# The gate's projection as seven half-size products over both halves of the tokens

## The chip, the cores and the metric

One core of a Trainium2 chip runs the whole kernel. The metric is the time of one execution in microseconds, median of several runs. Its engines are TensorE (PE), VectorE (DVE), ScalarE (ACT), GpSimd (POOL) and SyncE (SP), which here only issues transfers; each has its own instruction stream and they meet at semaphores.

## The reference

One layer of a decoder over 1024 tokens of 2048 features, in float32. Cut to what matters here:

```python
y = jnp.concatenate([y_h, y_g], axis=-1) @ w_out[i]
h = h + y.astype(dtype)

e = rms_norm(p[i] @ ple_proj[i], ple_norm_w[i])
gate = jax.nn.sigmoid(rms_norm(h, ple_gate_norm_w[i]) @ ple_gate_w[i] + ple_gate_b[i])
h = h + (gate * e).astype(dtype)
return rms_norm(h, final_norm_w)
```

Ahead of it stand an input projection and two groups of linear-attention heads. The change is in the last four lines: the projection with `ple_gate_w` (2048 x 2048), the gate, and the final norm.

## The kernel before

The tokens are worked on in two halves of 512; activations lie feature by feature, as tiles of 128 features x 512 tokens. `tile(h, c)` is tile c (of 16) of half h: in `feat` for half 0, in `work` for half 1. A product in float32 accuracy is made of three in a rounded format: both operands are split into a high part (by ScalarE: `split_weights`, `fill_high`) and a low part (by VectorE: `low_weights`, `fill_low`), and `passes` issues low x high, high x low, high x high. The operands stand in `act_hi`/`act_lo` and, twice, in `w_hi`/`w_lo`.

Weights come in slabs of 1 MB, in two transfers of 512 KB that SyncE issues (`load_slab`), each as soon as `low_weights` of the same half of the slab before has freed `w_raw[j]`. A slab is 16 x 3 = 48 products of 512 columns. The code of VectorE and ScalarE has in each iteration the splitting of the next slab first and then the work on the present one. The order on every engine is that of the code; SyncE's loads are in a written order too, so that a load which must wait holds up all behind it.

The output projection (`OUT_SLABS = 28`) is already made of seven half-size matrix products over both token halves (P1, P2, P5, P6, P7, P4, P3, four slabs each; a slab is two parts of 24 products, each into its own bank of four, `out_banks`). GpSimd makes the sums of weight blocks (`w_sums`) and of activations (`t_sums`) by transfers that add to their destination. `out_part` combines on VectorE; `x_part` brings in the residual from x tiles that SyncE loads (`load_x_tile`); `out_square` on ScalarE and `out_end` on VectorE add up the squares. `row_factors` makes a factor per token from these sums, at slabs 21, 25 and 27.

The gate's projection is 2 x 16 whole slabs, `g_pair` on TensorE: half 0, then half 1, one tile of logits per slab. For each tile VectorE runs `g_first` and `g_rest` (multiply by the row factor, add the bias, weights' low part, log-sigmoid with ScalarE's Abs, Exp, Ln and Exp, multiply by e, add to h, which stands in the tile, scale, add the square). SyncE loads e ahead (`load_e`), one slab early. The loops over half 1 scale half 0's tiles (`f_scale`) and store them (`store_out`). The last slab is made in two half-width parts; the tail (`z_...`) finishes it, makes the factors of half 1 and scales and stores that half, six tiles of it by token through TensorE's transposes.

## Time and profile before

| | us |
|---|---|
| median of 3 runs (2191.51 to 2192.65) | 2192.04 |
| span of the profiled execution, first to last instruction | 2189.4 |
| TensorE busy in it | 2175.6 |
| VectorE busy | 1520.5 |
| ScalarE busy | 1014.7 |

The profile's span leaves out what lies around the instructions; no time of its own is listed for the profiled execution, so its span is set against the median. A busy share is a mean over all stages. Start times count from the span's start; overlapping instructions of one kind in a row are merged, so that a price is best read as the distance between two starts.

### The profile page before, as it was taken

The numbers are of one execution on the slowest core, as the hardware profiler recorded it, in microseconds if no ns is written. First come the engines' busy times: TensorE is split into PE (matmuls) and PEld (weight loads), VectorE is DVE, ScalarE is ACT, GpSimd is POOL, SyncE is SP. The second block draws the span as 40 slices with busy tenths as digits, with TensorE's granted clock in tenths as the row PEclk, the third lists the DMA queues.
The fourth block names the chain that finished last, engine by engine and source line by source line (L and its number), as shares of the span: only waits on it lengthen the run. The fifth ranks groups of instructions, "written<-read, shape, count | busy, mean of one in ns | idle before, by whom it ended". The sixth has DMA issues, their size and how long they took to land.

```text
span 2189.4 us, 30587 instructions
## 1 busy us (share of the span) xinstructions
PE 2175.6 (99%) x10418; PEld 1821.7 (83%) x10418; DVE 1520.5 (69%) x3019; ACT 1014.7 (46%) x1759; POOL 96.8 (4%) x148
## 2 busy tenths in 40 slices
PE   9999999999999999999999999999999999999997
PEld 8888888888888888888888888888888888888886
DVE  7577777775666577766667565557667777768886
ACT  7454545444334354444445343335354445446554
POOL 1001011110000000000000000000110000000000
PEclk9999999999999999999999999999999999999998
DMA  9435665565432322232322545335576543332443
GB/s 338 170 102 163 171 178 168 165 177 145 125 99 86 97 69 87 85 126 81 115 99 93 173 152 141 98 108 145 187 250 235 173 163 115 121 123 98 159 161 127
DMA packets 100015, 310.27 MB, mean 142 GB/s; under 512 B 11360, under 2 KB 16736, under 8 KB 99168
## 3 DMA queue, kind: packets, MB, share of 16 engines
q1 hardware_dynamic: 88288, 248.42, 33.7%
q0 software_dynamic: 11648, 60.83, 10.9%
q8 instruction: 46, 0.75, 0.1%
q14 instruction: 33, 0.27, 0.0%
HBM read 284.04 MB, written 75.50 MB: 164 GB/s over the span
## 4 chain that ended last, share of the span: by engine, by line
PE 98%; DVE 1%; ACT 1%; issue 0%; DVEq 0%; ACTq 0%
PE acc L740 27%; PE acc L742 27%; PE acc L741 27%; PE lv L833 3%; PE so L842 1%; PE so L845 1%; PE so L822 1%; PE ms L742 1%; PE ms L741 1%; PE ms L740 1%; PE ms L811 1%; PE tr L741 1%; PE tr L742 1%; PE tr L740 1%; PE tr L857 0%; PE tr L807 0%
## 5 line engine op out<-in xcount | busy, mean ns | idle before, releaser
L740 PE MATMUL acc<-act_hi,w_lo 128*128 128x512 f32 (+1 forms) x2656 | 1063.0, 400 | 0.7 <-DVE work L2058 0.7
L742 PE MATMUL acc<-act_hi,w_hi 128*128 128x512 f32 (+1 forms) x2656 | 1033.9, 389 | 0.0
L741 PE MATMUL acc<-act_lo,w_hi 128*128 128x512 f32 (+1 forms) x2656 | 1033.4, 389 | 0.0
L742 PEld LDWEIGHTS acc<-act_hi,w_hi 128*128 128x128 f32 x2656 | 498.6, 188 | 104.9
L740 PEld LDWEIGHTS acc<-act_hi,w_lo 128*128 128x128 f32 x2656 | 499.7, 188 | 99.2 <-issue 3.9
L741 PEld LDWEIGHTS acc<-act_lo,w_hi 128*128 128x128 f32 x2656 | 500.0, 188 | 95.5 <-issue 1.7
L1049 ACT CAST w_hi<-w_raw 128x1024 fp32r<-128x1024 f32 x347 | 350.7, 1048 | 444.1 <-PE acc L742 357.5
L1537 DVE TENSOR_TENSOR w_lo<-w_raw,w_hi 128x1024 fp32r<-128x1024 f32 x347 | 410.7, 1220 | 104.4 <-ACT w_hi L1049 101.2
L1121 ACT ACTIVATE work<-work 128x512 f32<-128x512 f32 x120 | 75.7, 630 | 148.2 <-DVE work L1593 147.4
L1063 ACT ACTIVATE work<-work 128x512 f32<-128x512 f32 x95 | 60.1, 632 | 136.8 <-DVE work L1573 136.8
L1607 DVE COPY_PREDICATED work<-mask_sb,lv 128x256 f32<-128x256 uint8 x168 | 88.8, 529 | 7.3
L833 PEld LDWEIGHTS lv<-work 128*128 128x128 f32 x480 | 71.9, 190 | 9.4
L1599 DVE TENSOR_TENSOR work<-work 128x256 f32<-128x256 f32 x120 | 50.9, 424 | 39.4 <-ACT work L1121 39.3
L833 PE MATMUL lv<-work 128*128 128x128 f32 x480 | 72.6, 273 | 0.0
L1059 ACT ACTIVATE work<-work 128x512 f32<-128x512 f32 x103 | 65.2, 633 | 3.3
L1057 ACT ACTIVATE work<-work 128x512 f32<-128x512 f32 x103 | 65.2, 633 | 3.3
L1521 DVE MEMSET vec_dummy<- 128x1 f32 x230 | 13.6, 59 | 68.2 <-PE lv L833 63.5
L1578 DVE SCALAR_TENSOR_TENSOR work<-acc,work 128x512 f32<-128x512 f32 x48 | 33.2, 692 | 33.8 <-ACT work L1063 33.8
L1149 ACT ACTIVATE work<-work 128x128 f32<-128x128 f32 (+1 forms) x96 | 32.0, 334 | 41.5 <-DVE work L1642 41.5
L1593 DVE TENSOR_TENSOR work<-work 128x256 f32<-128x256 f32 x120 | 50.3, 419 | 0.0
L1592 DVE TENSOR_TENSOR work<-work 128x256 f32<-128x256 f32 x120 | 50.2, 419 | 0.0
L1600 DVE TENSOR_TENSOR work<-work 128x256 f32<-128x256 f32 x120 | 50.2, 418 | 0.0
(323 smaller groups left out, 2186.8 us busy)
## 6 DMA issues: line engine op xcount, KB each, us to landing
w_raw<-in_slabs SPq DMA_DIRECT2D x316, 512.0 KB, 4.5
w_sums<-in_slabs POOLq DMA_DIRECT2D x48, 512.0 KB, 6.3
w_raw<-w_sums SPq DMA_DIRECT2D x32, 512.0 KB, 4.2
work<-e_scratch SPq DMA_DIRECT2D x56, 256.0 KB, 2.8
t_sums<-y_scratch POOLq DMA_DIRECT2D x24, 512.0 KB, 6.8
feat<-in_x_feat SPq DMA_DIRECT2D x8, 1024.0 KB, 11.7
e_scratch<-work SPq DMA_DIRECT2D x32, 256.0 KB, 5.9
w_sums<-w_sums POOLq DMA_DIRECT2D x16, 512.0 KB, 3.9
```

The lines of the kernel that those rows point to most:

```text
L740: nc.tensor.matmul(ps, lhs_lo, rhs_hi, start=start, stop=False)
L741: nc.tensor.matmul(ps, lhs_hi, rhs_lo, start=False, stop=False)
L742: return nc.tensor.matmul(ps, lhs_hi, rhs_hi, start=False, stop=stop)
L833: last = nc.tensor.matmul(scores[:, :, c * half:(c + 1) * half], x_lv[l % 3][:, c * C:(c + 1) * C], queries[:, :, c * half:(c + 1) * half] ...
L1049: nc.scalar.copy(w_hi[par][:, j, :], w_raw[j][:, :]).then_inc(w_hi_ready, 1)
L1057: st.mark(A(t1, t1, ACT.Exp, scale=-1.0))
L1059: A(t1, t1, ACT.Ln, bias=1.0).then_inc(sp_ready, 1)
L1063: A(t2, t2, ACT.Exp).then_inc(sig_ready, 1)
L1121: A(x_lv[l % 3], x_lv[l % 3], ACT.Exp).then_inc(lv_exp, 1)
L1537: v.tensor_tensor(w_lo[par][:, j, :], w_raw[j][:, :], w_hi[par][:, j, :].bitcast(F32), ALU.subtract).then_inc(w_lo_ready, 1)
L1599: st.mark(v.tensor_tensor(keys, keys, lower_tokens(k_t, s), ALU.mult))
L1607: v.copy_predicated(upper_tokens(attn, s), mask_sb[:, l, :].rearrange("p (b n s) -> p b n s", b=2, s=s), lv_ps[l % 2][:, 0:TH // 2].rearra ...
```

## The change

The gate's projection becomes seven half-size products over both token halves as well: 28 slabs (`GATE_SLABS`) of two parts, in the order P1, P2, P1, P2 (two slabs each), then P6, P7, P5, P4, P3 (four each). A P2 slab finishes two tiles of half 0 (c below 8), P5 two of half 1 (c from 8), P4 two of half 0, P3 two of half 1; P1, P6 and P7 finish none. Weight sums for it (`weight_sums(1, c)`) are made by GpSimd during the input projection. The row factor is applied to the logits as before.

The tile of h is no longer kept in SBUF: as a tile of h is finished in the output projection, SyncE stores it (`keep_h`), ScalarE then multiplies it in place by the norm weight with a sign (`sign_tile`), and SyncE stores this too (`store_signed`); GpSimd makes four groups of sums of it (`G1` to `G4`). The gate loads these sums (`load_gate_t`, three buffers) and, for every tile, e and h (`load_tile`, two buffers). The gate's sigmoid is one Sigmoid with the bias in it, in place of four functions; ScalarE loads another function table for it and back for the row factors. The final scaling of half 0 and its sixteen stores stand behind the gate's loop; the final norm's weight is applied there instead of tile by tile.

```diff
+GATE_PARTS = ([(P1, 0), (P1, 1), (P2, 0), (P2, 1), (P1, 2), (P1, 3), (P2, 2), (P2, 3)]
+              + [(what, i) for what in (P6, P7, P5, P4, P3) for i in range(4)])
+def gate_tile(n, j):
+    what, i = GATE_PARTS[n]
+    c = 2 * i + j
+    return {P2: (0, c), P5: (1, HK + c), P4: (0, HK + c), P3: (1, c)}.get(what)
...
+            def keep_h(q):
+                h, c, n, j = OUT_TILES[q]
+                sp.wait_ge(out_free[out_place(n, j)], out_done(n))
+                if q >= 4:
+                    sp.wait_ge(*tile_stored(q - 4))
+                sp.dma_start(h_kept[h, c], (feat, work)[h][:, c, :]).then_inc(h_out[q % 4], 16)
+            def store_signed(q):
+                h, c = OUT_TILES[q][0:2]
+                sp.wait_ge(hs_ready, q + 1)
+                sp.dma_start(h_signed[h, c], (feat, work)[h][:, c, :]).then_inc(h_out[q % 4], 16)
+            def load_tile(q):
+                h, c = G_TILES[q][0:2]
                 if q >= 2:
-                    sp.wait_ge(e_used, q - 1)
-                sp.dma_start(e_in[c % 2], e_scratch[q]).then_inc(e_loaded[c % 2], 16)
+                    sp.wait_ge(g2_sum, q - 1)
+                sp.dma_start(e_in[q % 2], e_scratch[h * KT + c]).then_inc(e_loaded[q % 2], 16)
+                sp.dma_start(h_in[q % 2], h_kept[h, c]).then_inc(e_loaded[q % 2], 16)
+            def load_gate_t(a, k):
+                u = gate_use(a, k)
+                if k == 0 and a != 24:
+                    sp.wait_ge(gt_summed[a - 20], HK // 2 * 16)
+                if u >= 3:
+                    sp.wait_ge(act_lo_ready, FILL_NO[21] + u - 2)
+                src = h_signed[1, HK + k] if a == 24 else t_sums[a - 16, k]
+                sp.dma_start(gate_t[u % 3], src).then_inc(gt_loaded[u % 3], 16)
...
-                if n == 25:
-                    sp.wait_ge(act_lo_ready, fill_no(14, HK - 1))
-                    load_e(0, 0)
-                    load_e(0, 1)
+                for j in range(2):
+                    if (n - 1, j) in ENDS_AT:
+                        keep_h(ENDS_AT[n - 1, j])
+                for j in range(2):
+                    if (n - 2, j) in ENDS_AT:
+                        store_signed(ENDS_AT[n - 2, j])
                 load_slab(S_OUT + n + 3)
-            for h in range(HALVES):
-                for c in range(KT):
-                    if h * KT + c + 2 < 2 * KT:
-                        load_e(h + (c + 2) // KT, (c + 2) % KT)
-                    if s_gate(h) + c + 3 < SLABS:
-                        load_slab(s_gate(h) + c + 3)
-                    if h and 2 <= c < 10:
-                        store_out(0, 2 * c - 4)
-                        store_out(0, 2 * c - 3)
+            sp.wait_ge(logit_ready, HALVES * NG)
+            sp.wait_ge(glr_ready, HALVES)
+            sp.wait_ge(act_lo_ready, fill_no(14, HK - 1))
+            for n in range(GATE_SLABS):
+                if n == 0:
+                    for q in (30, 31):
+                        keep_h(q)
+                    for q in (28, 29, 30, 31):
+                        store_signed(q)
+                for j in range(2):
+                    if (n, j) in G_NO:
+                        load_tile(G_NO[n, j])
+                if n + 1 < GATE_SLABS:
+                    for a, k in GATE_FILLS_AT[n + 1]:
+                        load_gate_t(a, k)
+                if n == 4:
+                    sp.wait_ge(copied, 2 * HK * 64)
+                    sp.wait_ge(summed, 2 * HK * 64)
+                if n + 3 < GATE_SLABS:
+                    load_slab(S_GATE + n + 3)
+            for n in range(KT):
+                store_out(0, n)
+            T0, T1 = TOKEN_FIRST, TOKEN_FIRST + N_TOK
...
+            for c in range(HK // 2):
+                pool.wait_ge(y_stored, (HK + c) * 16 + 32)
+                weight_sums(1, c)
...
+            pairs = range(0, HK, 2)
+            for c in pairs:
+                hs_there(0, c)
+                g.dma_start(flat(G1, c, 2), flat(h_signed[0], c, 2)).then_inc(gt_copied, 16)
+            for c in pairs:
+                hs_there(1, c)
+                g.dma_start(flat(G3, c, 2), flat(h_signed[1], c, 2)).then_inc(gt_copied, 16)
+                pool.wait_ge(gt_copied, HK // 2 * 16 + c // 2 * 16 + 16)
+                add_to(flat(G1, c, 2), flat(h_signed[1], c, 2)).then_inc(added1, 16)
+            pool.wait_ge(added1, HK // 2 * 16)
+            for c in pairs:
+                g.dma_start(flat(G2, c, 2), flat(G1, c, 2)).then_inc(gt_copied, 16)
+            for c in pairs:
+                hs_there(1, HK + c)
+            pool.wait_ge(gt_copied, 3 * HK // 2 * 16)
+            for c in pairs:
+                add_to(flat(G2, c, 2), flat(h_signed[1], HK + c, 2)).then_inc(added2, 16)
+            for c in pairs:
+                add_to(flat(G3, c, 2), flat(h_signed[1], HK + c, 2)).then_inc(added3, 16)
+            pool.wait_ge(added2, HK // 2 * 16)
+            for c in pairs:
+                g.dma_start(flat(G4, c, 2), flat(G2, c, 2)).then_inc(gt_copied, 16)
+            for c in pairs:
+                hs_there(0, HK + c)
+            pool.wait_ge(gt_copied, 4 * HK // 2 * 16)
+            for c in pairs:
+                add_to(flat(G4, c, 2), flat(h_signed[0], HK + c, 2)).then_inc(added4, 16)
...
+            def sign_tile(n, j):
+                q = ENDS_AT[n, j]
+                h, c = OUT_TILES[q][0:2]
+                act.wait_ge(*tile_kept(q))
+                scale = (pgn if (h == 0) == (c < HK) else pgn_neg)[:, c:c + 1]
...
                 if (n - 1, 1) in ENDS_AT:
                     out_square(n - 1, 1)
+                    sign_tile(n - 1, 0)
                 if (n, 0) in ENDS_AT:
                     out_square(n, 0)
                 if out_slab(n)[0] in (P1, P5):
                     for j in range(2):
                         out_copy(n, j)
+                if (n - 1, 1) in ENDS_AT:
+                    sign_tile(n - 1, 1)
...
+            def g_sigmoid(q):
+                h, c = G_TILES[q][0:2]
+                act.wait_ge(logit_at, q + 1)
+                A(sig[q % 2], tile(h, c), ACT.Sigmoid, bias=g_vec[:, 3 * c:3 * c + 1]).then_inc(sig_ready, 1)
+            def g_square(q):
+                h, c = G_TILES[q][0:2]
+                act.wait_ge(g2_sum, q + 1)
+                A(sq[q % 2], tile(h, c), ACT.Square).then_inc(g2_sq, 1)
+                if h == 1 and TOKEN_FIRST <= c < TOKEN_FIRST + N_TOK:
+                    A(tile(h, c), tile(h, c), ACT.Copy, scale=g_vec[:, 3 * c + 2:3 * c + 3]).then_inc(fw_ready, 1)
+            for n in range(GATE_SLABS):
+                after = G_NO.get((n - 1, 1))
+                if n + 1 < GATE_SLABS and n:
+                    split_weights(S_GATE + n + 1, (n + 1) % 2, (0,))
+                if after is not None:
+                    g_sigmoid(after)
+                if n + 1 < GATE_SLABS and n:
+                    split_weights(S_GATE + n + 1, (n + 1) % 2, (1,))
+                if after is not None:
+                    g_square(after)
+                if n in (2, 27):
+                    act.preload_act_table_set("natural_log_exp_and_others")
+                    if n == 2:
+                        row_rsqrt(ROWS_H[1], r_h[1], h_sum[1])
+                    else:
+                        row_rsqrt(ROWS_F[0], f_r[0], g_sum[0])
+                    act.preload_act_table_set("sigmoid_and_others")
+                for a, k in GATE_FILLS_AT[n]:
+                    fill_high(a, k)
+                if GATE_PARTS[n][0] == P1:
+                    for j in range(2):
+                        p1_copy(n, j)
+                if (n, 0) in G_NO:
+                    g_sigmoid(G_NO[n, 0])
+                    g_square(G_NO[n, 0])
                 st.fresh()
...
+            def g_logits(n, j):
+                q = G_NO[n, j]
+                h, c = G_TILES[q][0:2]
+                vec_e.wait_ge(out_free[gate_place(n, j)], gate_freed(n))
+                st.wait()
+                v.tensor_tensor(tile(h, c), tile(h, c), r_h[h], ALU.mult).then_inc(logit_at, 1)
+            def g_embed(q):
+                h, c = G_TILES[q][0:2]
+                vec_e.wait_ge(e_loaded[q % 2], q // 2 * 32 + 32)
+                st.mark(v.scalar_tensor_tensor(out=e_in[q % 2], in0=e_in[q % 2], scalar=g_vec[:, 3 * c + 1:3 * c + 2], in1=r_e[h],
+                                               op0=ALU.mult, op1=ALU.mult))
+            def g_sum_up(q):
+                h, c = G_TILES[q][0:2]
+                vec_e.wait_ge(sig_ready, SIG_GATE + q + 1)
+                st.wait()
+                st.mark(v.tensor_tensor(e_in[q % 2], e_in[q % 2], sig[q % 2], ALU.mult))
+                st.wait()
+                v.tensor_tensor(tile(h, c), h_in[q % 2], e_in[q % 2], ALU.add).then_inc(g2_sum, 1)
+            def g_add(q):
+                h = G_TILES[q][0]
+                vec_e.wait_ge(g2_sq, q + 1)
+                v.tensor_tensor(g_sum[h], g_sum[h], sq[q % 2], ALU.add).then_inc(g2_ready, 1)
+                vec_e.wait_ge(g2_ready, q + 1)
+            def f_scale(n):
+                v.scalar_tensor_tensor(out=tile(0, n), in0=tile(0, n), scalar=g_vec[:, 3 * n + 2:3 * n + 3], in1=f_r[0],
+                                       op0=ALU.mult, op1=ALU.mult).then_inc(f_scaled, 1)
+            LAST = len(G_TILES) - 1
+            for n in range(GATE_SLABS):
+                after = G_NO.get((n - 1, 1))
+                if n + 1 < GATE_SLABS and n:
+                    low_weights(S_GATE + n + 1, (n + 1) % 2, (0,))
+                if after is not None:
+                    g_sum_up(after)
+                if n + 1 < GATE_SLABS and n:
+                    low_weights(S_GATE + n + 1, (n + 1) % 2, (1,))
+                if after is not None:
+                    g_add(after)
+                if n == 2:
+                    row_factors(ROWS_H[1], r_h[1], h_sum[1])
+                    st.mark(v.memset(g_sum[1], 0.0))
+                    st.wait()
+                elif n == 27:
+                    row_factors(ROWS_F[0], f_r[0], g_sum[0])
+                for a, k in GATE_FILLS_AT[n]:
+                    fill_low(a, k)
+                g_part(n, 0)
+                if (n, 0) in G_NO:
+                    g_logits(n, 0)
+                    g_embed(G_NO[n, 0])
+                    g_sum_up(G_NO[n, 0])
+                if n < GATE_SLABS - 1:
+                    g_part(n, 1)
+                    if (n, 1) in G_NO:
+                        g_logits(n, 1)
+                        g_embed(G_NO[n, 1])
+                if (n, 0) in G_NO:
+                    g_add(G_NO[n, 0])
+                if n < GATE_SLABS - 1:
+                    st.fresh()
...
+            for u in range(0, 6):
+                f_scale(u)
             z_variance(0)
-            z_logs(1)
             z_factor(0)
-            z_gate(1)
-            z_scale(0, N_TOK, N_TOK + 4)
             z_variance(1)
-            z_scale(0, N_TOK + 4, N_TOK + 6)
             z_factor(1)
-            z_scale(0, N_TOK + 6, KT)
-            z_scale(1, N_TOK, KT)
+            for u in range(6, KT):
+                f_scale(u)
+            z_scale(0, 0, KT - N_TOK)
+            z_scale(1, 0, KT - N_TOK)
```

Where it moves instructions. On VectorE an iteration of the gate had one tile; this is one of half 1, from its logits to the spacer (`g_t`, `g_m` are in `work`, `restart_sb` holds e's factor, `state_g` the squares):

```order
L2058 TENSOR_TENSOR work<-acc,state_h 128x512 [waits acc_ready]
L2061 TENSOR_SCALAR work<-work,gv_now 128x512 [waits vec_steps,acc_free1]
L1537 TENSOR_TENSOR w_lo<-w_raw,w_hi 128x1024 [waits w_hi_ready]
L2070 SCALAR_TENSOR_TENSOR work<-work,gv_now,restart_sb 128x512 [waits e_loaded1]
L1573 SCALAR_TENSOR_TENSOR work<-work 128x512 [waits vec_steps,sp_ready]
L2075 TENSOR_TENSOR work<-work 128x512 [waits sig_ready]
L2077 TENSOR_TENSOR work<-work 128x512
L2079 TENSOR_SCALAR work<-work,gv_now 128x512 [waits g2_sum]
L2083 TENSOR_TENSOR state_g<-state_g,work 128x512 [waits g2_sq]
L1521 MEMSET vec_dummy 128x1 [waits vec_steps,g2_ready]
```

Now an iteration of P3 on VectorE, second tile of the slab before first (`glr_r` and `glr_all` are the two buffers of h):

```order
L1720 TENSOR_TENSOR w_lo<-w_raw,w_hi 128x1024 [waits w_hi_ready]
L2292 TENSOR_TENSOR work<-work 128x512 [waits sig_ready]
L2294 TENSOR_TENSOR work<-glr_all,work 128x512 [waits vec_steps]
L1720 TENSOR_TENSOR w_lo<-w_raw,w_hi 128x1024 [waits w_hi_ready]
L2300 TENSOR_TENSOR state_g<-state_g,work 128x512 [waits g2_sq]
L2270 TENSOR_TENSOR work<-work,tr 128x512 [waits tr_free,acc_ready,g2_ready]
L2278 TENSOR_TENSOR work<-work,state_h 128x512 [waits vec_steps,tr_free]
L2284 SCALAR_TENSOR_TENSOR work<-work,vecs,restart_sb 128x512 [waits e_loaded0]
L2292 TENSOR_TENSOR work<-work 128x512 [waits vec_steps,sig_ready]
L2294 TENSOR_TENSOR work<-glr_r,work 128x512 [waits vec_steps]
L2270 TENSOR_TENSOR work<-work,ms 128x512 [waits ms_free,acc_ready]
L2278 TENSOR_TENSOR work<-work,state_h 128x512 [waits vec_steps,ms_free]
```

So two tiles stand in one slab, and the loads that `L2284` waits for serve this very slab. On SyncE, in the first half of the gate before, the load of e stood ahead of a pair of weight loads:

```order
L588 DMA work<-e_scratch 128x512 [waits e_used]
L492 DMA w_raw<-in_slabs 128x1024 [waits w_lo_ready] x2
L588 DMA work<-e_scratch 128x512 [waits e_used]
L492 DMA w_raw<-in_slabs 128x1024 [waits w_lo_ready] x2
```

Now, in P4, four loads for the tiles, two of sums, and the weight pair; and at the end all stores of half 0 ahead of those of half 1:

```order
L668 DMA work<-e_scratch 128x512 [waits g2_sum]
L669 DMA glr_r<-h_kept 128x512
L668 DMA work<-e_scratch 128x512 [waits g2_sum]
L669 DMA glr_all<-h_kept 128x512
L679 DMA x_lv<-h_signed 128x512 [waits act_lo_ready]
L679 DMA state_h<-h_signed 128x512 [waits act_lo_ready]
L557 DMA w_raw<-in_slabs 128x1024 [waits w_lo_ready] x2
```

```order
L683 DMA out<-feat 128x512 [waits f_scaled] x16
L738 DMA out<-work 128x4x256 [waits tok_scaled]
L738 DMA out<-work 128x2x256 [waits tok_scaled]
L743 DMA out<-work 128x2x256 [waits f_scaled] x5
```

The weight pair waits for `low_weights` of the iteration in which the next loads are used; the sixteen stores were in the gate's loop. On ScalarE, in the output projection, the scaling in place (`L1522`) now stands between the squares (`L1514`) and ahead of the next slab's cast; it waits for the store of its tile (`h_out`):

```order
L1514 ACTIVATE work<-feat 128x512 [waits h_added,ms_free]
L1522 ACTIVATE feat<-feat,vecs 128x512 [waits h_out2]
L1514 ACTIVATE work<-work 128x512 [waits h_added,acc_free0]
L1522 ACTIVATE feat<-feat,vecs 128x512 [waits h_out3]
L1202 COPY act_dummy<-vecs 128x1
```

Before, only the two squares stood there.

## Rows read from the trace of the kernel before

**Rows 1.** The page, part 1: busy us, share of the span, instructions.
```profile
PE 2175.6 (99%) x10418; PEld 1821.7 (83%) x10418; DVE 1520.5 (69%) x3019; ACT 1014.7 (46%) x1759; POOL 96.8 (4%) x148
```

**Rows 2.** Windows, the tail: length, busy us of each engine, granted clock, DMA.
```profile
2170.60:2189.40 18.80, 7.33 (x50) 6.24 (x48) 11.46 (x41) 6.95 (x17) 0.00 (x0) 0.68 0.67 224
```

**Rows 3.** Time line of TensorE around the first gate slab: start us, us.
```profile
1829.69 0.39 PE L742 MATMUL acc<-act_hi,w_hi 128*128 128x512 f32 x1
...
1842.39 0.39 PE L741 MATMUL acc<-act_lo,w_hi 128*128 128x512 f32 x1
```

**Rows 4.** Time line of VectorE in one slab of the output projection.
```profile
1764.64 2.36 DVE L1537 TENSOR_TENSOR w_lo<-w_raw,w_hi 128x1024 fp32r<-128x1024 f32 x2
1766.92 1.29 DVE L1945 TENSOR_TENSOR feat<-state_h,feat 128x512 f32<-128x512 f32 x2
1768.12 1.29 DVE L1553 TENSOR_TENSOR act_lo<-work,act_hi 128x512 fp32r<-128x512 f32 x2
...
1775.32 0.06 DVE L1521 MEMSET vec_dummy<- 128x1 f32 x1
1775.52 2.36 DVE L1537 TENSOR_TENSOR w_lo<-w_raw,w_hi 128x1024 fp32r<-128x1024 f32 x2
```

**Rows 5.** Time line of VectorE in one gate tile.
```profile
2143.83 0.69 DVE L2075 TENSOR_TENSOR work<-work 128x512 f32<-128x512 f32 x1 [0.70 <-ACT work L1063]
2144.67 0.69 DVE L2077 TENSOR_TENSOR work<-work 128x512 f32<-128x512 f32 x1
...
2146.06 0.69 DVE L2083 TENSOR_TENSOR state_g<-state_g,work 128x512 f32<-128x512 f32 x1 [0.18 <-ACT work L1438]
...
2146.93 0.17 DVE L2056 COPY gv_now<-vecs 128x3 f32 x1 [0.18 <-DVE state_g L2083]
```

**Rows 6.** Time line of VectorE: row factors, then six fills.
```profile
1789.58 0.69 DVE L1543 TENSOR_SCALAR so<-so 128x512 f32<-128x512 f32 x1
...
1794.34 1.29 DVE L1943 TENSOR_TENSOR work<-work,state_h 128x512 f32<-128x512 f32 x2
...
1822.27 4.06 DVE L1556 SCALAR_TENSOR_TENSOR act_lo<-feat,vecs,act_hi 128x512 fp32r<-128x512 f32 x6 [1.44 <-ACT act_hi L1107]
```

**Rows 7.** DMA issues of the whole run: count, KB each, median us to landing.
```profile
work<-e_scratch SPq DMA_DIRECT2D x56, 256.0 KB, 2.8
state_h<-in_x_feat SPq DMA_DIRECT2D x32, 256.0 KB, 5.0
y_scratch<-work SPq DMA_DIRECT2D x16, 256.0 KB, 2.0
t_sums<-t_sums POOLq DMA_DIRECT2D x8, 512.0 KB, 4.8
```

**Rows 8.** The same view, 1740 to 1800 us.
```profile
state_h<-in_x_feat SPq DMA_DIRECT2D x10, 256.0 KB, 4.3
```

**Rows 9.** Time line of SyncE's queue: a slab of the output projection; the last stores.
```profile
1756.93 1.46 SPq L492 DMA_DIRECT2D w_raw<-w_sums  x2
1758.66 0.94 SPq L577 DMA_DIRECT2D state_h<-in_x_feat  x2
...
2175.28 1.52 SPq L631 DMA_DIRECT2D out<-work  x2
...
2182.15 4.34 SPq L635 DMA_DIRECT2D out<-work  x5
```

**Rows 10.** Time line of VectorE in the tail: second token factor to next scaling.
```profile
2177.03 0.15 DVE L2155 TENSOR_SCALAR small<-ms 128x2 f32<-128x2 f32 x1
...
2179.15 1.41 DVE L2174 TENSOR_TENSOR work<-work,acc 128x256 f32<-128x256 f32 x4
```

**Rows 11.** Time line of ScalarE between two slabs of the output projection.
```profile
1753.71 0.63 ACT L1346 ACTIVATE work<-feat 128x512 f32<-128x512 f32 x1 [5.00 <-DVE sq_sum L1977]
1754.25 0.17 ACT L1035 COPY act_dummy<-vecs 128x1 f32<-128x1 f32 x1
1754.59 2.00 ACT L1049 CAST w_hi<-w_raw 128x1024 fp32r<-128x1024 f32 x2 [0.17 <-ACT act_dummy L1035]
```

479 lines of the change are left out of this document (233 added, 246 removed).

## The prediction

> **What bounds it now.** I read the busy shares first: TensorE is busy 2175.6 of 2189.4 us, VectorE only 69% [rows 1]. The stages in windows come next: at the full granted clock to the end of the gate's last product, then 18.8 us in which TensorE has 7.3 us of work: the tail [rows 2]. The time line of TensorE gives the price of a product: 56 steps in 12.70 us, 0.2268 us each, back to back [rows 3]. So a half or a whole slab of 24 or 48 products takes 5.44 or 10.88 us, and today every saved product is saved time, as long as VectorE, ScalarE and the queues deliver within a slab. Whether they still do is the question.
>
> **What is removed.** 32 whole slabs (1536 products of 512 columns) become 28 (1344). 192 x 0.2268 = **43.5 us less**. The stage now runs from 2170.6 - 32 x 10.88 = 1822.5 us; it would be TensorE's for 304.6 instead of 348.2 us.
>
> **VectorE in the last twelve slabs (P5, P4, P3).** Before, one slab finishes one tile. Now the first sixteen slabs finish 8 tiles and the last twelve finish 23 and a half: two a slab. The prices, start to start [rows 4 to 6]: a low half of weights 1.14 us, a plain 512-column operation 0.60, a scalar_tensor_tensor 4.06/6, about 0.66; the multiplication by the sigmoid to the sum behind it 0.84; the sum to the addition of its square, over ScalarE, 1.39; that addition to the next operation 0.87; the spacer 0.20. The logit to its sigmoid and back has the same shape as sum to square, I take 1.40, and 0.72 for an operation whose own semaphore is awaited. An iteration of P3 in code order: low half 1.14, late tile 0.84 + 0.60, low half 1.14, square 0.87, first tile 0.72 + 1.40 + 0.84 + 0.60, second tile 0.72 + 0.60 + 0.66, square and spacer 1.07: **11.2 us**. P4 has two fills more, 12.4; P5 also a second operation on each bank, 13.6. All are over TensorE's 10.88.
>
> **The load in front of each first tile.** SyncE issues the tile's e and h only behind the slab load that waits for this iteration's second low half (the order shows it). That half is done 1.14 + 1.44 + 1.22 = 3.8 us after the iteration's start; a load issued behind a slab pair leaves 0.6 us after it and the next 0.6 later (1758.66 against 1756.93, whose second load is 1.14 in) [rows 9]. So h leaves at 5.0. What it takes is between 2.8 us (the e loads of now, alone) and 5.0 (x tiles behind slab loads, whole run) [rows 7]; the quiet stretch of that same pattern shows 4.3 [rows 8], which I take, since here h has a slab half and e in front of it. It lands at 9.3. The first embed operation is due at 5.9 in P3, and 5.3 us of the iteration stand behind it: the iteration becomes 9.3 + 5.3 = **14.6 us**, in P4 too, and 15.2 in P5. With 2.8 us it is 13.1 and 13.7, with 5.0 15.3 and 15.9. The embed operation's semaphore counts both loads, e's and h's, so it waits for the later.
>
> The Trainium skill (DMA: Bandwidth & Descriptors, Anatomy of one DMA) makes a transfer about 2.0 us and bytes over 436 GB/s. By that estimate h, with slab half and e in front, lands at 3.9 + 2.0 + 2.4 = 8.3 us, and an iteration is 13.6: the forecast would be 11 us lower. The lone loads of the trace, 2.8 us, stand near its 2.6.
>
> Iteration 16 has no late tile and waits for TensorE: it ends 15 us after slab 16 starts. From there three times 15.2 (17 to 19) and six times 14.6 (20 to 25): iteration 26 starts at 148.2. TensorE may start slab n+1 when iteration n has its first low half, 1.3 us in. Slab 27 starts at 149.5 instead of 11 x 10.88 = 119.7: **29.8 us lost** (about 15 with 2.8 us loads, 10 with no wait at all). The lateness is first eaten by some 6 us of slack, so TensorE should stall from slab 20 on.
>
> **The tail.** Iteration 27 starts 14.6 us after 26, 13.3 into slab 27. On VectorE then: late tile and its square 2.2, row factors 0.9 + 4.76 [rows 6], tile (27,0) 0.72 + 1.40 + 0.84 + 1.39, square and embed 1.5: 13.7. The half-width last tile: two products and two gates, some 3.8: 17.5. Six scalings of half 0 at 0.66, 21.5; two token factors at 2.1 [rows 10], 25.7; ten scalings, 32.3. These sixteen were inside the gate stage before. SyncE's fourteen last stores stand in its order behind all sixteen of half 0: 2175.28 to 2186.49 is 11.2 us for the same fourteen, and 2.9 to the end [rows 9]. Sum 46.4. From the nominal end of slab 27 that is 13.3 + 46.4 - 10.9 = 48.8 us against 18.8: **30.0 us more**. The scalings and the stores are certain; the bounds are 25 and 34.
>
> ScalarE also switches function tables in this chain. No row prices it; the Trainium skill (ScalarE: Activation LUTs, What ACT_TABLE_LOAD costs) says about 2.7 us a switch, which by that estimate would put 1 us onto the row factors; the others stand beside VectorE's scalings.
>
> **The out stage.** Each finished tile is stored (h_kept), then scaled in place by ScalarE, which waits for that store, then stored again (h_signed). In ScalarE's order the first scaling stands ahead of the square of the next tile and of the next slab's cast. Let a be VectorE's start into a slab, now 1.6 us. SyncE issues the store behind slab pair and x pair, at a + 4.1 [rows 9]. A store alone takes 2.0 us [rows 7]; behind four loads I take 4.3 to 4.9, landing near a + 9.0. Then scaling, square, scaling at 0.54 each, the spacer 0.34 and a cast 1.04 [rows 11]: the next low half starts at a + 12.2, which is a + 1.3 in the next slab. It drifts by 1.3 us a slab from slab 17 on; under 3.6 us for the store it doesn't. The row factors of slabs 21 and 25 stand ahead of the x tiles and add 5 each. The slack ends at a = 9.6. So 1.6 + 4 x 1.3 + 5 = 11.9 in slab 22, then 3 x 1.3 + 5 + 1.3: **12 us lost**, between 0 and 18. The sign scalings themselves, two of 0.54 a slab, are nothing on ScalarE, busy 46%.
>
> **The start of the gate.** The first sum needed is G2. Its last inputs are stored some 12 us into the stage; then a copy, an addition, four copies and four additions in a row on GpSimd's queue, at 4.8 us for one [rows 7]; four at once I put at 10: about 42 us, needed at 5.3 slabs, 58. Hidden, with 16 us to spare. But the eight fills of slabs 6 and 7 share three buffers and SyncE waits for them ahead of slab 9 and of tiles 7: three load-and-fill turns put iteration 8 some 14 us into its slab, **4 us** over the slack, 0 to 10. GpSimd's eight more weight sums run beside the input projection as the first eight do, under a TensorE that is never idle there: nothing; if a slab came late, some us each.
>
> **The sum.** 2189.4 - 43.5 + 29.8 + 30.0 + 12 + 4 = 2221.7 us of span. The shown median lies 2.6 above the profiled span: **2224 us**, 1.5% slower.
>
> **Rivals.** (a) As above with no drift in the out stage, the stores landing within 3.6 us: 2224 - 12 = 2212, less 4 if G is smooth: 2208. For it: the 2.0 us stores; against: nothing in front of those. (b) G2 or the hand-over between the stages is late as well: if the out stage ends with a near 9.6, the casts for gate slab 1 slip by 6 to 8 us, and G2, some 8 us later as well, may cost up to as much again once its copies are slower than put: 2231 to 2248. (c) Loads at 2.8 us, no drift: 2192.0 - 43.5 + 15 + 28.5 = 2192, no change. (d) The other side, faster: VectorE is never kept waiting by e and h. Then the iterations are 13.6, 12.4 and 11.2, slab 27 is 10 us late and the tail 28 longer: 2192.0 - 43.5 + 10 + 28 = 2186.5; below it only with a shorter tail, down to 2180. What decides is the landing of h: under 2.3 us behind its issue it costs about nothing in P4 and P5. No row of now has a load of that size this fast. (e) That the products are not saved: they are counted in the code, no chance.
>
> **Chances.** The sum as made, 0.45; (a) 0.28; (b) 0.10; (c) 0.06; (d) 0.11. Range: from (a)'s lower side to (b)'s lower half, 2198 to 2243. A measurement can tell about 0.2% (4 us) from no change. Slower by more 0.83, within 0.05, faster 0.12.
>
> **What would show it.** TensorE's idle time, now nil to 2170, should stand in gate slabs 20 to 27 (2 to 4 us each) behind w_lo, and in out slabs 22 to 27. VectorE's embed operation should show waits of 1.5 to 3.5 us released by the h or e transfer. The sixteen stores of half 0 should all be issued within the last 35 us, and the last fourteen stores in a row at 0.8 us each. I am wrong if the embed operations don't wait, if iterations in P3 pass in 11 us, or if the tail behind the last product is under 35 us.

## The result, and the profile after

The changed kernel takes 2293.1 us (median of 4 runs, 2292.8 to 2293.6) beside 2192.4 us of the kernel before on the same chip (4 runs, 2191.5 to 2195.7): ratio 1.0458, 95% interval 1.0446 to 1.0470, slower. The forecast was 2224 with a range from 2198 to 2243. The sign was right, the size was not: 101 us came instead of 32.

The page after: busy time, one line of the slices, and the traffic. Against [rows 1] TensorE's busy time is only 6.5 us less, though the saved products are worth 43.5. So the loss is not waiting alone. The last run below (c9) has the same 10202 products in 2138.5 us instead of 2169.1. The difference, 30.6 us, is in the main what products lost by running at a lower granted clock. I put this at 25 to 30 of the 101 us: an estimate, since the modelled end of a product ahead of a gap adds some 0.16 us each time.

```profile
PE 2169.1 (95%) x10202; PEld 1805.3 (79%) x10202; DVE 1505.9 (66%) x2976; ACT 995.7 (43%) x1742; POOL 161.2 (7%) x244
...
PEclk9999999999999999999999999999999898899996
...
DMA packets 126905, 392.20 MB, mean 171 GB/s; under 512 B 14816, under 2 KB 20320, under 8 KB 125280
```

The stages after, in windows whose edges are starts of slabs on TensorE: out slabs 9 to 19, out slabs 20 to 27, gate slabs 0 to 9, 10 to 15, 16 to 26, and from slab 27's start to the end. Columns as in [rows 2]: length, busy time of TensorE (and count), of its weight loads, of VectorE, ScalarE and GpSimd, the granted clock, the DMA share, GB/s.

```profile
1620.76:1747.90 127.14, 122.55 (x529) 100.93 (x530) 89.98 (x130) 64.26 (x110) 11.84 (x22) 0.97 0.69 238
1747.90:1861.75 113.85, 98.98 (x392) 77.72 (x390) 65.16 (x99) 45.18 (x73) 5.66 (x11) 0.93 0.64 219
1861.75:2019.92 158.17, 120.78 (x482) 96.39 (x483) 84.14 (x123) 58.40 (x91) 18.97 (x27) 0.89 0.76 228
2019.92:2085.20 65.28, 65.28 (x289) 54.07 (x288) 29.70 (x42) 18.84 (x30) 0.00 (x0) 1.00 0.44 149
2085.20:2235.12 149.92, 127.45 (x532) 102.00 (x530) 118.47 (x175) 60.23 (x93) 0.00 (x0) 0.97 0.49 169
2235.12:2290.70 55.58, 22.63 (x120) 20.51 (x120) 43.26 (x89) 16.49 (x30) 0.00 (x0) 0.66 0.52 180
```

A slab without a wait is 10.88 us. So ten gate slabs should be 108.8 us and are 158.2; eleven should be 119.7 and are 149.9; of these stages only slabs 10 to 15 run at 10.88 throughout. The account of the span, 2189.4 to 2290.7: products -43.5; the gate starts at 1861.8 instead of 1822.5, **+39.3** (forecast 12); gate slabs 0 to 9 **+49.4** (forecast 4); slabs 16 to 26 **+30.2** (forecast 29.8); the tail, 55.6 us from slab 27's start where 10.9 + 18.8 stood, **+25.9** (forecast 30.0). The sum is 101.3. Two of the four terms came within about 4 us; the other two are 73 us over their forecast, and the tail is 4 under.

*Out stage.* Issues of the h_kept stores on SyncE, then the scalings on ScalarE that wait for them and the cast behind; first in out slab 5, then twice in the late slabs.

```profile
1573.86 0.85 SPq L655 DMA_DIRECT2D h_kept<-feat  x2
...
1748.62 1.11 SPq L655 DMA_DIRECT2D h_kept<-work  x2
1763.13 0.96 SPq L655 DMA_DIRECT2D h_kept<-work  x2
```

```profile
1585.43 0.72 ACT L1522 ACTIVATE feat<-feat,vecs 128x512 f32<-128x512 f32 x1 [13.57 <-DMA h_kept<-feat]
...
1755.63 0.72 ACT L1522 ACTIVATE work<-work,vecs 128x512 f32<-128x512 f32 x1 [8.55 <-DMA h_kept<-work]
...
1758.02 2.00 ACT L1216 CAST w_hi<-w_raw 128x1024 fp32r<-128x1024 f32 x2 [0.17 <-ACT act_dummy L1202]
1770.18 0.72 ACT L1522 ACTIVATE work<-work,vecs 128x512 f32<-128x512 f32 x1 [8.59 <-DMA h_kept<-work]
```

The scaling starts 7.0 us behind the issue of the store (1748.62 to 1755.63), where the forecast had 4.3 to 4.9, and 11.6 in slab 5. The cast stands behind it, and the cycle from one scaling to the same in the next slab is 14.6 us.

*Start of the gate.* VectorE, GpSimd and TensorE around gate slab 4, which is 27.95 us long. The last column in brackets is the idle time before and what ended it.

```profile
1937.63 0.75 DVE L2284 SCALAR_TENSOR_TENSOR work<-work,vecs,r_e 128x512 f32<-128x512 f32 x1 [14.14 <-DMA glr_r<-h_kept]
...
1945.69 1.23 DVE L1720 TENSOR_TENSOR w_lo<-w_raw,w_hi 128x1024 fp32r<-128x1024 f32 x1
```

```profile
1909.37 2.04 POOL L876 DMA_DIRECT2D t_sums<-t_sums  x4 [4.59 <-DMA t_sums<-h_signed]
1919.88 6.75 POOL L768 DMA_DIRECT2D t_sums<-h_signed  x8 [8.48 <-DMA t_sums<-t_sums]
1939.68 1.98 POOL L886 DMA_DIRECT2D t_sums<-t_sums  x4 [13.05 <-DMA t_sums<-h_signed]
```

```profile
1947.06 0.77 PE L897 MATMUL tr<-act_hi,w_lo 128*128 128x512 f32 x1 [16.81 <-DVE w_lo L1720]
1947.62 0.63 PE L898 MATMUL tr<-act_lo,w_hi 128*128 128x512 f32 x1
...
1951.89 0.63 PE L899 MATMUL tr<-act_hi,w_hi 128*128 128x512 f32 x1
1952.32 0.43 PE L897 MATMUL tr<-act_hi,w_lo 128*128 128x512 f32 x1
```

The tile's h, issued at 1922.31, is in use at 1937.6, while GpSimd has eight additions of 512 KB each in flight. VectorE's next low half of weights stands behind that operation and the second tile's, which waits as well, and TensorE stands idle for 16.8 us. Then twelve products take 5.26 us instead of 2.72. Windows of TensorE alone (length, busy time, granted clock, DMA share) show why: ahead of the gap, in its first and second part, at the slow products and behind them.

```profile
1919.10:1930.00 10.90, 10.89 (x48) 1.00 0.86 194
1930.30:1935.00 4.70, 0.00 (x0) 1.00 1.06 244
1935.00:1947.00 12.00, 0.00 (x0) 0.51 1.08 242
1947.06:1952.32 5.26, 5.26 (x13) 0.50 1.01 395
1952.40:1960.00 7.60, 7.60 (x35) 1.00 0.55 170
```

The clock is granted at its lower level, 1.2 of 2.4 GHz, in the second part of the gap and still at the twelve products, and this gap costs 2.5 us more than its length.

*The last twelve slabs.* One iteration of VectorE in P3, from its first low half to the first embed operation to the next iteration's first low half:

```profile
2204.62 1.23 DVE L1720 TENSOR_TENSOR w_lo<-w_raw,w_hi 128x1024 fp32r<-128x1024 f32 x1
...
2213.89 0.75 DVE L2284 SCALAR_TENSOR_TENSOR work<-work,vecs,restart_sb 128x512 f32<-128x512 f32 x1 [3.53 <-DMA glr_r<-h_kept]
...
2219.02 1.23 DVE L1720 TENSOR_TENSOR w_lo<-w_raw,w_hi 128x1024 fp32r<-128x1024 f32 x1
```

The embed starts 9.3 us into the iteration, the iteration is 14.4 us: forecast 9.3 and 14.6.

### The profile page after: what moved, and what is told of

The parts are those of the page before. It is cut to its first block, busy times and chain, and to the rows that moved or that the text cites. A ratio compares the mean times of both kernels' runs of the same rounds, so it can differ in the third digit from the quotient of the medians.

```text
span 2290.7 us, 30047 instructions
## 1 busy us (share of the span) xinstructions
PE 2169.1 (95%) x10202; PEld 1805.3 (79%) x10202; DVE 1505.9 (66%) x2976; ACT 995.7 (43%) x1742; POOL 161.2 (7%) x244
## 4 chain that ended last, share of the span: by engine, by line
PE 72%; DVE 12%; DMA 10%; ACT 3%; issue 2%; SPq 1%; DVEq 0%; ACTq 0%
PE acc L897 20%; PE acc L899 20%; PE acc L898 20%; DVE w_lo L1720 4%; PE lv L990 3%; DMA glr_r<-h_kept 3%; DMA h_kept<-feat 3%; DMA w_raw<-in_slabs 2%; DMA h_kept<-work 2%; PE so L999 1%; PE so L1002 1%; PE so L979 1%; ACT w_hi L1216 1%; DVE work L2284 1%; DMA glr_all<-h_kept 1%
## 5 line engine op out<-in xcount | busy, mean ns | idle before, releaser
L897 PE MATMUL acc<-act_hi,w_lo 128*128 128x512 f32 x2376 | 963.4, 405 | 46.9 <-ACT w_hi L1216 18.5
L899 PE MATMUL acc<-act_hi,w_hi 128*128 128x512 f32 x2376 | 931.9, 392 | 0.0
L898 PE MATMUL acc<-act_lo,w_hi 128*128 128x512 f32 x2376 | 931.6, 392 | 0.0
L1289 ACT ACTIVATE work<-work 128x512 f32<-128x512 f32 x120 | 75.8, 632 | 147.8 <-DVE work L1776 147.2
L897 PE MATMUL tr<-act_hi,w_lo 128*128 128x512 f32 x192 | 80.7, 420 | 39.5 <-DVE w_lo L1720 39.5
L1230 ACT ACTIVATE work<-work 128x512 f32<-128x512 f32 x64 | 40.5, 633 | 95.2 <-DVE work L1756 95.2
L897 PEld LDWEIGHTS tr<-act_hi,w_lo 128*128 128x128 f32 x192 | 38.6, 201 | 52.4 <-issue 44.5
L899 PE MATMUL tr<-act_hi,w_hi 128*128 128x512 f32 x192 | 78.7, 410 | 0.0
L898 PE MATMUL tr<-act_lo,w_hi 128*128 128x512 f32 x192 | 78.6, 409 | 0.0
L1782 DVE TENSOR_TENSOR work<-work 128x256 f32<-128x256 f32 x120 | 50.9, 424 | 39.3 <-ACT work L1289 39.3
L897 PE MATMUL ms<-act_hi,w_lo 128*128 128x512 f32 (+1 forms) x192 | 73.8, 385 | 0.0
L898 PE MATMUL ms<-act_lo,w_hi 128*128 128x512 f32 (+1 forms) x192 | 73.8, 385 | 0.0
## 6 DMA issues: line engine op xcount, KB each, us to landing
feat<-in_x_feat SPq DMA_DIRECT2D x8, 1024.0 KB, 12.2
```

Of the source, the lines that this page charges most:

```text
L897: nc.tensor.matmul(ps, lhs_lo, rhs_hi, start=start, stop=False)
L898: nc.tensor.matmul(ps, lhs_hi, rhs_lo, start=False, stop=False)
L899: return nc.tensor.matmul(ps, lhs_hi, rhs_hi, start=False, stop=stop)
L1230: A(t2, t2, ACT.Exp).then_inc(sig_ready, 1)
L1289: A(x_lv[l % 3], x_lv[l % 3], ACT.Exp).then_inc(lv_exp, 1)
L1782: st.mark(v.tensor_tensor(keys, keys, lower_tokens(k_t, s), ALU.mult))
```

## The experiments

Each run tells time, then by stage: start of the gate, gate slabs 0 to 9, slabs 16 to 26, slab 27's start to the end. The kernel before took 2191.0 us beside e1 to e4, 2191.9 beside e5, e6 and c1 to c6, 2191.7 beside c7 to c9. Runs with a range are medians of several, the others single runs; the stages are those of one profiled execution each. In e5 the gate starts 2.9 us later than in the changed kernel, though nothing ahead of it was changed: a difference of 3 us in a stage of two single runs proves nothing.

```
run                       us                        gate at  0-9    16-26  tail
after                     2293.1                    1861.8   158.2  149.9  55.6
e1_no_gate_sums           2262.8                    1861.2   129.2  149.2  56.1
e2_sign_later             2246.1                    1820.0   153.1  148.6  56.1
e3_tiles_early            2254.5                    1860.5   145.0  126.8  55.1
e4_sums_spread            2288.2                    1875.9   142.4  147.2  55.6
e5_tail                   2302.6                    1864.7   160.8  149.0  61.0
c1_sign_tiles             2208.9                    1821.0   139.2  126.8  54.8
c2_sign_tiles_sums        2205.1                    1818.7   137.5  126.8  54.9
c3_all                    2218.8 (2209.1-2222.8)    1819.8   147.4  128.1  58.4
c4_four_buffers           2207.0                    1820.4   137.8  126.8  54.9
c5_sums_four_buffers      2199.7                    1820.0   130.8  126.8  54.9
c6_sums_delayed           2201.1 (2198.8-2203.4)    1819.5   131.8  126.8  54.9
e6_four_buffers_no_sums   2183.9                    1819.8   115.4  126.8  54.8
c7_sums_interleaved       2189.3 (2186.0-2195.1)    1819.8   120.5  126.8  54.9
c8_stores_split           2187.6 (2185.1-2191.5)    1821.0   118.5  126.8  55.0
c9_last_signs_later       2187.8 (2185.7-2192.7)    1822.5   116.8  126.8  55.0
```

### One edit at a time

**e1_no_gate_sums.**

```
-            for c in pairs: ... (all copies and additions for G1 to G4)
-                    sp.wait_ge(gt_summed[a - 20], HK // 2 * 16)
-                src = h_signed[1, HK + k] if a == 24 else t_sums[a - 16, k]
+                src = h_signed[1, HK + k]
```

> GpSimd's transfers that form the gate's operand sums (16 copies and 16 additions of tile pairs) are left out, and the gate's fills read h_signed tiles in their place, so the gate's values are not the reference's; everything else stays. Theory TRAFFIC (the bulk transfers of GpSimd delay the small loads and stores of SyncE): the 28 us gate slab 4 falls to under 14 us, gate slabs 0 to 9 together from 158 to under 125 us, and the run from 2293 to 2250 to 2265. Theory ORDER (it is the places in SyncE's and ScalarE's programs, not the load on the queues): slab 4 stays over 20 us and the run at 2280 or more. Both expect the late out slabs 20 to 23 at 15 us as they are, since none of these transfers runs there.

2262.8 us. Slab 4 is 13.1 us, slabs 0 to 9 are 129.2, 4 over the bound named; the late out slabs are as before. TRAFFIC holds. The transfers issued between 1920 and 1960, first after, then in this run (KB each, median us to landing):

```profile
w_raw<-in_slabs SPq DMA_DIRECT2D x4, 512.0 KB, 9.4
```

```profile
w_raw<-in_slabs SPq DMA_DIRECT2D x4, 512.0 KB, 3.6
```

The same weight loads in the same stage take 9.4 us beside the additions and 3.6 without them (medians of four), and the tile's h 15.3 and 7.3. The run also leaves out SyncE's wait for the sums. In the changed kernel that wait held up nothing: G2's additions have landed when GpSimd issues G4's copies at 1939.7, and the first load of G2 leaves at 1960.7.

**e2_sign_later.**

```
                 if (n - 1, 1) in ENDS_AT:
                     out_square(n - 1, 1)
-                    sign_tile(n - 1, 0)
...
-                if (n - 1, 1) in ENDS_AT:
-                    sign_tile(n - 1, 1)
+                for j in range(2):
+                    if (n - 2, j) in ENDS_AT:
+                        sign_tile(n - 2, j)
```

> ScalarE scales each finished tile one slab later, at the end of its iteration, and SyncE stores it one slab later (eight semaphores for the stores instead of four). Theory SIGN (the scaling waits in ScalarE's order for the h_kept store, ahead of the next cast): out slabs 20 to 27 fall from 114 us together to 90 at most, the 13.6 and 7.7 us waits of slabs 4 to 8 are gone, the gate starts by 1830 instead of 1862, and the run is near 2260. Rival WORK (VectorE's and ScalarE's own operations don't fit into 10.88 us): out slabs 20 to 27 stay over 13 us each and the run over 2280.

2246.1 us, 47 less. Out slabs 20 to 27 in the window of this run, against 113.85 us above:

```profile
1730.20:1820.00 89.80, 89.80 (x392) 73.24 (x391) 66.98 (x101) 46.31 (x76) 4.09 (x8) 1.00 0.81 279
```

The DMA share is higher than before the edit and TensorE never waits: the load on the queues does no harm here once no engine stands behind a store. The gate starts at 1820.0. SIGN holds, WORK falls.

**e3_tiles_early.**

```
+            def load_slab_and_tiles(n):
+                m = n + 1
+                if (m, 0) in G_NO:
+                    load_tile(G_NO[m, 0])
+                for j in range(2):
+                    if n + 3 < GATE_SLABS:
+                        load_half(S_GATE + n + 3, j)
+                    if j == 0 and (m, 1) in G_NO:
+                        load_tile(G_NO[m, 1])
```

> SyncE issues the loads of the next iteration's first tile (e, h) ahead of the first weight load that it waits for, and those of the second tile between the two weight loads. Theory BEHIND THE SLAB LOAD (my step on the last twelve slabs): the embed operation no longer waits for the first tile, an iteration is 13.6, 12.4 and 11.2 us, slab 27 starts some 20 us earlier after slab 16 (130 instead of 150 us), and the run is near 2272. Rival WORK: it stays at 14.3 us a slab. Rival TRANSFER: the wait moves to the second tile's load, and 8 us or less are won.

2254.5 us. Slabs 16 to 26:

```profile
2070.80:2197.60 126.80, 121.88 (x532) 99.08 (x531) 118.84 (x177) 60.36 (x93) 0.00 (x0) 1.00 0.60 195
```

23.1 us less than 149.9, no embed operation waits, slabs 16 to 19 are 10.88 us and 20 to 26 11.0 to 12.5: what is left over 10.88 is VectorE's own work, but for 0.9 us of row sums on TensorE in slab 26. BEHIND THE SLAB LOAD holds. The other 15 us came from elsewhere: slab 4 is 12.6 instead of 28 us. The same eight additions are issued, from 1920.4 on, but the first tile's loads now leave ahead of them and not behind, and the embed operation starts at 1922.9. Slab 7 rose to 25.9.

```profile
1914.42 0.32 SPq L668 DMA_DIRECT2D work<-e_scratch  x1
1914.78 0.48 SPq L669 DMA_DIRECT2D glr_r<-h_kept  x1
```

**e4_sums_spread.**

```
+            for c in pairs:
+                hs_there(1, c)
+                plus(flat(G2, c, 2), flat(H[1], c, 2), added2)
+                pool.wait_ge(added2, (4 + c // 2 + 1) * 16)
```

> GpSimd forms the gate sums from the tiles in the order in which they are finished, so that only additions of half-1 tiles are left when the last tile is stored, and they go one pair at a time (G2's, then G3's, G1's, G4's) instead of eight at once; two more additions a pair than before. Theory BURST (what delays the tile loads is the number of bulk transfers at once): the embed operation's 14 us wait in gate slab 3 falls to 4 at most, gate slab 4 to under 17 us, and the run to 2260 to 2275. Theory VOLUME (their bytes count, however they are spread): the stall is spread as well, and the run stays within 8 us of 2293. Rival LATE SUM: G2 one at a time is not ready at gate slab 6, TensorE waits there by 5 us or more.

2288.2 us. Slabs 0 to 9 became 15.8 us shorter, slab 4 is 16.7, but an embed operation beside slab 4 still waits 5.8 us, over BURST's bound of 4, and the time as a whole lies within VOLUME's 8 us of 2293. So BURST holds in its own place alone. But the gate starts 14 us later: the spread transfers now run in out slabs 24 to 27, whose stores ScalarE waits for. The volume did not vanish (it grew: 24 additions instead of 16); it moved to the next engine that stands behind a transfer.

**e5_tail.**

```
+                if h == 0:
+                    A(tile(h, c), tile(h, c), ACT.Copy, scale=g_vec[:, 3 * c + 2:3 * c + 3]).then_inc(fw0_ready, 1)
...
+            for n in range(KT):
+                nc.gpsimd.tensor_tensor(tile(0, n), tile(0, n), f_r[0], ALU.mult).then_inc(f0_scaled, 1)
```

> One part alone, the tail: ScalarE multiplies each half-0 tile by its column vector right after its square, the row factor of half 0 is formed in iteration 26 instead of 27, GpSimd multiplies the sixteen tiles by it, and VectorE's sixteen scalings (0.66 us each) are gone, so that the half-0 stores leave before the last products' chain ends. Theory TAIL (scalings and stores stand in a row at the end): slab 27's start to the end falls by 13 to 15 us, of which the row factors give about 5 back in front of slab 27, and the run falls by 8 to 10, to about 2284. Rival SHARED: GpSimd's multiplications slow VectorE's operations beside them, and less than 3 us are won or some are lost.

2302.6 us, 9.5 more; the tail itself 5.4 more. SHARED is right. VectorE while GpSimd multiplies, then GpSimd's sixteen in a row:

```profile
2252.66 1.63 DVE L2302 TENSOR_TENSOR work<-glr_r,work 128x512 f32<-128x512 f32 x1
2254.22 0.67 DVE L2278 TENSOR_TENSOR work<-work,acc 128x512 f32<-128x512 f32 x1
...
2257.59 1.76 DVE L2308 TENSOR_TENSOR state_g<-state_g,work 128x512 f32<-128x512 f32 x1
```

```profile
2247.48 26.41 POOL L897 TENSOR_TENSOR feat<-feat,state_h 128x512 f32<-128x512 f32 x16 [282.48 <-DVE vec_dummy L2332]
```

The two operations with both operands in SBUF go from 0.69 to 1.63 and 1.76 us; the one with an operand in PSUM (`acc`) stays at 0.67. The Trainium skill (SBUF — State Buffer, Who interferes with whom) says that a VectorE instruction with two SBUF inputs contends with a GpSimd instruction that reads SBUF; the trace agrees, with 0.9 and 1.1 us for these two.

### Together

**c1_sign_tiles** (e2 and e3).

> The later scaling (alone 47 us) and the earlier tile loads (alone 39 us) together. If the two act in different stages, their gains add: 2293 - 86 = 2207 at best. If part of both is the same stall at the start of the gate (gate slabs 3 to 8, where GpSimd's transfers are in flight), 10 to 15 us of it are counted twice: 2217 to 2222.

2208.9 us: 84.2 less where the parts alone gave 47.0 and 38.6. They add.

**c2_sign_tiles_sums** (c1 and e4).

> As c1_sign_tiles, with the gate sums spread out as in e4_sums_spread, which alone won 20 us in the gate's start and lost most of it again in out slabs 24 to 27, where the scaling waited longer for its store. Theory: with the scaling off that path the loss is gone and the gain stays, so it is 8 to 16 us under c1. Rival VOLUME: the same bytes delay the same loads, and it is within 4 us of c1 or over it.

2205.1 us, 3.8 under c1. The loss in the out stage is gone (gate at 1818.7), as the theory said, but in gate slabs 0 to 9 only 1.7 us are won: by its bound of 4 us, VOLUME. Slabs 3, 4 and 7 are 11.5 us shorter, slabs 1, 2, 8 and 9 some 9.9 longer.

**c3_all** (c2, the tail of e5, and the fourth fill load of slabs 6 and 7 behind the weight loads).

```
+                    for a, k in GATE_FILLS_AT[n + 1][0:3]:
...
+                if n + 1 < GATE_SLABS:
+                    for a, k in GATE_FILLS_AT[n + 1][3:]:
+                        load_gate_t(a, k)
```

> As c2, with the tail of e5_tail, and with the fourth gate fill's load of slabs 6 and 7 issued behind the tile and weight loads, which in e3_tiles_early waited 17 us in SyncE's order for a buffer of the fill. If these add to c2: 8 to 10 us for the tail and 5 to 10 for slab 7, so about 2190, which is no clear gain over the kernel before. Rival: what bounds slabs 6 to 8 is the contention itself, and it is 2200.

2218.8 us, ratio to the kernel before 1.0109 (1.0081 to 1.0138): a miss. Slab 7 rose from 18.0 to 31.4 us, where the fill's last load now stands behind the weight loads and ScalarE waits 4.6 and 7.7 us for the last two fills; and the tail is slower, as in e5.

**c4_four_buffers** (c1 and a fourth fill buffer).

```
-        gate_t = [state_g[:, TH:2 * TH], x_lv2[:, :], state_h[:, TH:2 * TH]]
+        gate_t = [state_g[:, TH:2 * TH], x_lv2[:, :], state_h[:, TH:2 * TH], state_g[:, 0:TH]]
```

> c1_sign_tiles with a fourth buffer for the gate's fills (the unused sum tile of half 1, up to gate slab 15). In c1 gate slabs 7 and 8 are 23.3 and 17.8 us long: ScalarE waits for fill loads 7.4, 4.3 and 3.0 us long, and SyncE gets the fourth load of slab 7 out only once iteration 7 has freed its buffer, with tile and weight loads behind it. Theory BUFFERS: slabs 7 and 8 together fall from 41 to under 30 us, the run from 2209 to 2193 to 2199. Rival TRAFFIC (each load takes 5 to 8 us while GpSimd's eight additions are in flight, whatever the buffers): under 5 us are won.

2207.0 us, 1.9 less; slabs 7 and 8 are 39.6 instead of 41.1 us. BUFFERS falls, at least alone.

**c5_sums_four_buffers** (c4 and e4).

> c2_sign_tiles_sums (gate sums spread) with the fourth buffer. By BUFFERS 8 to 16 us under c2's 2205, and by up to 4 us under c4; by TRAFFIC within 5 us of c2.

2199.7 us, 5.3 under c2 and 7.3 under c4: between the bounds of the two theories, so it decides for neither.

**c6_sums_delayed.** GpSimd waits for slab 7's fills ahead of the additions for G1 and G4.

```
+                if dst is G1:
+                    pool.wait_ge(act_lo_ready, fill_no(21, HK - 1))
```

> c5 with the eight additions for G1 and G4, which are needed from gate slab 12 on, started only when slab 7's fills are done; G2's and G3's stay. By TRAFFIC gate slabs 3 to 8 lose at least half of what they still have over 10.9 us in c5, and the run is 4 to 8 us under it, at or under the kernel before (2192): 2184 to 2194. By BUFFERS alone it is equal to c5.

2201.1 us, ratio 1.0044 (1.0027 to 1.0061): no gain over c5, so the additions for G1 and G4 are not what stalls slab 7. The row that told why, ScalarE at the first fill with G2, for which TensorE's slab 7 is drawn out:

```profile
1912.21 0.62 ACT L1305 CAST act_hi<-state_g 128x512 fp32r<-128x512 f32 x1 [11.08 <-DMA state_g<-t_sums]
```

The last addition for G2 was issued at 1904.2: G2 is late. GpSimd, in program order, starts the gate's sums only behind the out stage's last fill loads.

**e6_four_buffers_no_sums** (c4 without the gate sums).

> c4 without GpSimd's gate sums (the gate's fills read h_signed tiles, so the gate's values are not the reference's). What gate slabs 0 to 9 are still over 108.8 us here is not traffic but order: by ORDER over 15 us, by TRAFFIC under 8. The run is then 2185 at the most by TRAFFIC.

2183.9 us. Slabs 0 to 9 are 115.4 us, 6.6 over nominal, all in slabs 0 to 2 (0.9 of it row sums on TensorE): TRAFFIC, by its bound of 8. The sums' whole price in c4 was 22 us.

**c7_sums_interleaved.** The same bytes as c6, earlier in GpSimd's order, and no longer each pair waited for before the next.

```
             for a in GROUPS[1:]:
                 for k in range(HK):
                     load_t(a, k)
+                    if a == 12 and k % 2 == 0:
+                        hs_there(0, k)
+                        for dst in (G1, G2):
+                            g.dma_start(flat(dst, k, 2), flat(H[0], k, 2)).then_inc(gt_copied, 16)
+                    if a == 14 and k >= 2 and k % 2 == 0:
+                        sum_p7(k - 2)
```

> c6 (later scaling, earlier tile loads, four buffers, spread sums) with GpSimd's gate sums moved forward in its own program: the copies of half-0 tiles stand between the loads for out slabs 12 to 15's fills, the additions of P7's tiles between those of slabs 20 to 23, G4's copies right behind, and behind the last tile only G2's four additions stand ahead of G3's. The bytes are the same. Theory GPSIMD ORDER (G2 is late by its place in the queue): ScalarE's 11 us wait for the G2 load is gone, gate slab 7 falls from 18.8 to under 12 us, and the run from 2201 to 2184 to 2190. Rival TRAFFIC: the same bytes, moved, stall slabs elsewhere, and the run stays at 2197 or more.

2189.3 us, ratio to the kernel before 0.9989 (0.9980 to 0.9998). Slab 7 is 10.9 us; the last addition for G2 is issued at 1864.0, 40 us earlier than in c6, and the same cast as above no longer waits:

```profile
1863.95 0.90 POOL L792 DMA_DIRECT2D t_sums<-h_signed  x1 [8.63 <-DMA t_sums<-h_signed]
```

```profile
1901.79 0.62 ACT L1304 CAST act_hi<-state_g 128x512 fp32r<-128x512 f32 x1
```

```profile
1819.82:1940.32 120.50, 114.41 (x483) 93.38 (x482) 82.43 (x122) 59.31 (x93) 9.86 (x12) 0.96 0.83 233
```

GPSIMD ORDER holds; the DMA share is 0.83 here, more than the changed kernel's 0.76, and yet slabs 2 to 9 have no stall. What is over 108.8 us, 11.7, is all in slabs 0 and 1.

**c8_stores_split** (c7, the sixteen half-0 stores on GpSimd's queue).

> c7 with the sixteen stores of half 0 issued on GpSimd's queue, so that SyncE's fourteen others don't stand behind them. Theory QUEUE (the tail ends with stores that had to queue behind sixteen others): 3 to 5 us are won, since VectorE ends at 8 us before the end and the last five stores take 4.5 us from there. Rival VECTOR (VectorE's chain of 36 scalings ends the kernel): under 1.5 us.

2187.6 us, ratio 0.9981 (0.9971 to 0.9990), 1.7 us under c7 with overlapping intervals, and the tail did not move (54.9 and 55.0). QUEUE falls, VECTOR is not refuted.

**c9_last_signs_later.** The last two scalings behind the casts for gate slab 2.

> c8 with the sign scalings of the last out slab's two tiles behind ScalarE's casts for gate slab 2 instead of ahead of them. Theory: gate slabs 0 to 2 (12.6, 14.0 and 12.6 us without sums, 45 us in c6) lose 3 to 6 us, and G2, now 8 us later, still comes before slab 6. Rival: the next wait (w_raw for slab 3, behind the last h_signed stores in SyncE's order) takes their place and the time stays within 2 us.

2187.8 us, ratio 0.9984 (0.9975 to 0.9993), the same as c8. Slab 0 fell from 17.7 to 15.4 us, slab 1 rose from 13.6 to 14.3 and the gate started 1.5 later: the rival, by its bound of 2 us. Slab 1 has no wait in it any more:

```profile
1837.90:1852.20 14.30, 14.26 (x50) 11.22 (x51) 5.90 (x10) 8.19 (x13) 0.81 (x1) 0.81 0.84 277
```

TensorE is busy from its start to its end, at a granted clock of 0.81, behind a gap of 4.4 us at the end of slab 0. Of its 3.4 us over 10.88, 0.9 are further products for the row factors (slab 26 has the same, at the full clock, and is 11.8 us) and 2.5 are the clock's.

## Why the prediction went wrong

**What is removed: right.** The slabs without waits are 10.88 us, and in e2 the gate starts at 1820.0 (forecast 1822.5 without losses).

**The last twelve slabs: right in mechanism and size.** 29.8 forecast, 30.2 measured. e3 took the load's place away and got 23.1 back; the forecast priced the same at 20 (29.8 to 10). What is left, 7.1, is nearly all VectorE's work, as in rival (d). The prediction's estimate by the Trainium skill (DMA: Bandwidth & Descriptors, Anatomy of one DMA), h landing at 8.3 us, would have been some 10 us too low here (the prediction says 11): the embed operation that waits for h starts at 9.3. That section gives its sum for transfers issued by GpSimd; these are SyncE's.

**The tail: right in mechanism, 4 us too large.** From the start of iteration 27 (2244.4, its spacer) to the end are 46.3 us, forecast 46.4. The term "iteration 27 starts 13.3 into slab 27" was mis-sized: it starts 9.3 in. The tile loads of iterations 26 and 27 have no weight load ahead of them any more, and iteration 26 took 10.8 us, not 14.6. The table switch stands in this trace at 1.28 us and the next operation begins right behind it:

```profile
2259.98 1.28 ACT L1690 ACT_TABLE_LOAD   x1
2261.28 0.72 ACT L1671 ACTIVATE state_g<-work 128x256 f32<-128x256 f32 x2
```

The prediction cited the Trainium skill (ScalarE: Activation LUTs, What ACT_TABLE_LOAD costs) for 2.7 us a switch, which is a load of 1.28 and a drain of 1.38. The trace agrees with the load; it shows no drain here, and the row factors took 4.7 us, as forecast from rows, without a microsecond on top.

**The out stage: the right wait, mis-sized: 12 against 39.** The step "behind four loads I take 4.3 to 4.9" failed in two ways. The store takes about 7 us, so the cycle is 14.6 us instead of 12.2. A likely reason is that [rows 7, 8] priced transfers of a kernel that moves 310 MB and this one moves 392, part of it here; no run tested it, and e1, without GpSimd's sums, has the same late out slabs. And the step looked only from slab 17 on; the same wait stands in slab 5, where the store takes 11.6 us. Against e2, slabs 6 to 10 are 17.7 us longer and slabs 20 to 27 24.1, together the 41.8 by which its gate starts earlier; some 9 of these are the lower clock's (98.98 against 89.80 us of TensorE's time for the same 392). e2 shows that all of it hangs on the scaling's place in ScalarE's order. (The prediction's 11.9 for 1.6 + 4 x 1.3 + 5 should be 11.8; nothing rests on it.)

**The start of the gate: the step that failed.** "Hidden, with 16 us to spare" put the sums at nothing, and it failed twice.

First, it did not ask what those transfers do to others. e1 and e6 put the sums' price at 29 us in the changed kernel and 22 us in c4. Loads beside them land late (h after 15.3 against 7.3 us), and an engine stands directly behind the load; e3 took most of slab 4's stall away without touching GpSimd, by sending the tile's loads off before the additions.

Second, its own time was wrong. G2 was to be there 42 us into the stage and needed at 58. Its additions landed at 1939.7, 78 us in. That the first load of G2 did not wait for them is luck: the stage was so late by then that the load left at 99 us. Once the other stalls were gone, G2 did come too late, by its place in GpSimd's order: c6 and c7 differ by 12 us.

**Rival (b)** named the place and stopped at 2248. It added the new waits, but priced each at the transfer times of the kernel before. The hand-over that it names, "slip by 6 to 8 us", is there: slab 0 is 8.2 us over.

**A term that was nowhere in the sum:** a gap in TensorE's work can cost more than its length. It was 2.5 us at slab 4 and, by the busy times above, some 25 to 30 of the 101 us in all. It goes away with the gaps, so it is contained in what each run gave back, and no run changed it by itself.

**Still open:** slabs 0 to 2 of the gate: 5 us over nominal in c1 and c4, 6.6 in e6 without the sums, 8 to 13 in the runs that spread them, and c9, which shortened them, gained nothing in all; why the store of the out stage takes 7 us; and the tail, 55 to 56 us in all but two of the runs, of which neither GpSimd's hands nor a second store queue took any.

## What to carry to other kernels

A sum over bulk transfers has two prices: when its result is ready, and what its bytes do to every small transfer that an engine stands behind; ask the second for each wait in the stage, with the durations of the crowded rows, not of the quiet ones. When a stage is crowded, first move the waiting instruction or the load's place in its queue (here 47 and 39 us by two reorderings, no byte less), then the producer's place in its own queue. Spreading transfers alone moved the stall to the next such place.

The seven-product form saves 43.5 us of TensorE's time here, and at first it cost 145 us elsewhere. Reordering and a fourth fill buffer took back 104 of these. Some 40 remain in c9: 25 in the tail, 8 in gate slabs 0 and 1, and 7 in slabs 16 to 26, nearly all VectorE's own work. So it ends 0.1 to 0.2% under the kernel before, about what can be told from no change.

## What the runs showed of the hardware

- After an idle gap of 16.8 us, TensorE's next twelve products started 0.44 us apart, then 0.23, with a granted clock of 0.50 (1.2 GHz) and then 1.00 (2.4 GHz). In slabs with gaps of about 1 us (e3, slabs 20 to 26) the granted clock stayed at 1.00. A slab without any wait, behind a gap of 4.4 us, took 14.3 instead of 11.8 us at 0.81 (c9).
- Two VectorE operations with both operands in SBUF took 1.63 and 1.76 us instead of 0.69 while GpSimd ran 128x512 multiplications (e5); one with an operand in PSUM took 0.67.
- With eight accumulating transfers of 512 KB in flight all queues together moved 242 to 244 GB/s, at a DMA share of 1.06 to 1.08, and a 512 KB weight load took 9.4 us instead of 3.6.
- A switch of ScalarE's function table took 1.28 us; the next operation began 0.02 us behind it.
